# Four column groups of the modulation product: one feature tile and 2048 columns at a time, instead of four feature tiles and 512 columns

## What is computed

```python
mod = jax.nn.silu(c) @ prm['w_ada'][l] + prm['b_ada'][l]
sh1, sc1, g1, sh2, sc2, g2 = jnp.split(mod[:, None, :], 6, axis=-1)
u = x * (1 + sc1) + sh1
...
x = layer_norm(DEEPNORM_ALPHA * x + (1 + g1) * m, ...)
u = x * (1 + sc2) + sh2
```

## Time and profile before

| | us |
|---|---|
| three runs | 1398.95, 1401.20, 1403.52 |
| median | 1401.20 |
| span of the profiled execution (first to last instruction) | 1398.4 |
| TensorE busy in it | 1350.5 (97%) |
| DVE, ACT, POOL busy | 816.9, 572.0, 45.3 |
| 48 loads of `w_ada`, 1 MB each, median time to landing | 7.0 |

### The profile page before, as it was taken

The page is one execution under the profiler, slowest core; times in us unless marked ns, Lnnn a source line. Parts: engine busy times, 40 slices in busy tenths (PEclk is TensorE's granted clock), DMA queues, the critical chain, the costliest instruction groups (busy, mean ns, idle before and its releaser), DMA issues.

```text
span 1398.4 us, 21871 instructions
## 1 busy us (share of the span) xinstructions
PE 1350.5 (97%) x9104; PEld 1132.9 (81%) x9104; DVE 816.9 (58%) x1275; ACT 572.0 (41%) x754; POOL 45.3 (3%) x102
## 2 busy tenths in 40 slices
PE   7999999989999999999999999999999999999996
PEld 3678777879999986788877899999977787877673
DVE  1567216564444446663265843654655668999896
ACT  2361113163433324521232543333344546677762
POOL 6000003000000000000200000000000000000000
PEclk9899999999999999999999899999999999999998
DMA  9643773775544553438342553743756769999991
GB/s 319 209 150 121 249 238 124 252 235 164 169 153 156 174 170 107 150 121 260 107 153 68 188 167 102 223 151 124 223 161 216 228 211 301 316 349 357 332 338 53
DMA packets 205301, 275.87 MB, mean 197 GB/s; under 512 B 7815, under 2 KB 136097, under 8 KB 205204
## 3 DMA queue, kind: packets, MB, share of 16 engines
q1 hardware_dynamic: 193216, 263.62, 57.1%
q10 hardware_dynamic: 11988, 10.86, 2.6%
HBM read 268.16 MB, written 6.30 MB: 196 GB/s over the span
## 4 chain that ended last, share of the span: by engine, by line
PE 92%; DVE 4%; ACT 1%; DMA 1%; issue 1%; SPq 0%; DVEq 0%; ACTq 0%
PE bank L1173 14%; PE bank L981 11%; PE bank L983 11%; PE bank L982 11%; PE bank L1011 7%; PE bank L1013 7%; PE bank L1012 7%; PE bank L1051 4%; PE bank L1122 3%; PE bank L1268 2%; PE bank L1280 2%; PE bank L1137 1%; PE bank L1276 1%; PE bank L1514 1%; PE bank L1085 1%
## 5 line engine op out<-in xcount | busy, mean ns | idle before, releaser
L748 DVE TENSOR_TENSOR lo_raw<-raw,hi 128x2048 fp32r<-128x2048 f32 (+2 forms) x112 | 229.3, 2055 | 99.6 <-ACT hi L1762 60.9
L1762 ACT ACTIVATE hi<-raw 128x2048 fp32r<-128x2048 f32 (+2 forms) x112 | 193.4, 1727 | 113.7 <-PE bank L1013 78.3
L1173 PE MATMUL bank<-UM,raw 128*128 128x288 f32 x864 | 219.4, 410 | 0.0
L981 PE MATMUL bank<-UH,hi 128*128 128x288 f32 x704 | 210.2, 299 | 4.8 <-DVE UL L2178 4.4
L983 PE MATMUL bank<-UL,hi 128*128 128x288 f32 x704 | 207.9, 295 | 0.0
L1173 PEld LDWEIGHTS bank<-UM,raw 128*128 128x128 f32 x864 | 163.3, 192 | 47.4 <-issue 4.6
L2190 DVE TENSOR_TENSOR lo<-raw,hi 128x2048 fp32r<-128x2048 f32 (+1 forms) x42 | 94.1, 2240 | 83.4 <-ACT hi L1975 48.5
L981 PEld LDWEIGHTS bank<-UH,hi 128*128 128x128 f32 x704 | 132.9, 189 | 5.4 <-issue 4.5
L983 PEld LDWEIGHTS bank<-UL,hi 128*128 128x128 f32 x704 | 133.5, 190 | 0.0
L982 PE MATMUL bank<-UH,lo 128*128 128x288 f32 x432 | 128.4, 297 | 0.0
L1011 PE MATMUL bank<-hi,UGH 128*128 128x512 f32 (+9 forms) x288 | 111.7, 388 | 0.0
(11 more groups left out here) (463 smaller groups left out, 2523.8 us busy)
## 6 DMA issues: line engine op xcount, KB each, us to landing
raw<-in_w_ada_dram SPq DMA_DIRECT2D x48, 1024.0 KB, 7.0
raw<-in_w_in_dram SPq DMA_DIRECT2D x28, 1024.0 KB, 8.2
raw<-in_w_exp_gate_dram SPq DMA_DIRECT2D x26, 1024.0 KB, 5.5
raw<-in_w_exp_up_dram SPq DMA_DIRECT2D x26, 1024.0 KB, 7.0
raw<-in_w_exp_down_dram SPq DMA_DIRECT2D x16, 1024.0 KB, 5.1
raw<-in_w_exp_down_dram SPq DMA_DIRECT2D x16, 768.0 KB, 4.8
raw<-in_w_ff_gate_dram SPq DMA_DIRECT2D x11, 1024.0 KB, 5.4
raw<-in_w_ff_up_dram SPq DMA_DIRECT2D x11, 1024.0 KB, 5.3
```

Source lines behind the costliest of these rows:

```text
L748: dve.tensor_tensor(lo_x[g % XRAW][:, 0:XG[g][2] * XG[g][3]], x_raw(g), hi_x[g % XSPLIT][:, 0:XG[g][2] * XG[g][3]].bitcast(F32), ALU.subtr ...
L981: pe.matmul(out, wh, xh, start=start, stop=False)
L1173: mm = pe.matmul(bank[t][:, 0:N], w_[:, d, t * P:t * P + P], UM[:, d, :], start=(d == 0), stop=(d == KT - 1))
L1762: act.activation(hi_x[q][:, 0:XG[g][2] * XG[g][3]], x_raw(g), ACT.Copy).then_inc(S("x_hi_made"), 1)
```

## The change

The column groups now take 512 columns each and the same feature tile. For a block of 2048 columns (four values of c) eight loads bring one feature tile of 128 rows each (rows of 8 KB in HBM); every load gives four products, one for each group, and bank 4 gathers them over all eight loads (four `ada` steps). Then one copy by ACT and one `adaT` of four plain transposes against the identity follow, and four operations of DVE pick the nine values of each group. `ada_ends` says which `ada` step is the last of its block; only it has a copy and an `adaT`.

The first block (layer 0, c 0 to 3) is `paired`: a step loads one half of the features for 512 columns of the shift and the same 512 of the scale, and waits for both loads before its products; two groups take each kind, with different feature tiles. After two steps the partial sums are added and turned by products with `sel2`, two copies of `sel`'s halves beside each other (18 columns), which DVE makes ahead of its first step. The order of the first four is 0, 1, 2, 3, and each pair has one `adaT` behind it.

Since bank 4 is now held across steps, also across the dense network, that network's going down uses the bank pairs (0, 1) and (7, 5). In layer 1 the `ada` step (1,10) moves from behind `lnm` to ahead of the last `wo` block (behind `wo 2`), (1,11) moves from behind `lnv` to its place between `lnm` and `lnv`, and the `adaT` of (1,11) stands behind `lnv` and ahead of `nu`. The number of loads, their bytes and the number of products at L1122 stay.

```diff
@@ -171,2 +171,12 @@
 
+def paired(l, c):
+
+    return (l, c // 4) == (0, 0)
+
+
+def ada_ends(l, c):
+
+    return c % 2 == 1 if paired(l, c) else c % 4 == 3
+
+
 def steps_of():
@@ -175,3 +185,3 @@
     s = [('start',), ('params',)]
-    early = [(0, c) for c in (0, 2, 1, 3, *range(4, ADA_CB))] + [(1, c) for c in range(4)]
+    early = [(0, c) for c in range(ADA_CB)] + [(1, c) for c in range(4)]
     late = [(1, c) for c in range(4, ADA_CB)]
@@ -187,3 +197,4 @@
                 s.append(('ada', *a))
-                last.append(a)
+                if ada_ends(*a):
+                    last.append(a)
 
@@ -329,4 +340,3 @@
         s += [('su', l, 1), ('sm', l, 1), ('wo', l, 2, 0), ('sa', l, 1), ('wo', l, 2, 1)]
-        if l == 0:
-            more_ada()
+        more_ada()
         one('sd_out')
@@ -337,6 +347,3 @@
         flush()
-        if l == 1:
-            more_ada()
         s += [('nu', l, 0), ('u', l, 1)]
-        flush()
         if l == 0:
@@ -373,3 +380,3 @@
     if k == 'ada':
-        return one(4)
+        return one(4) if ada_ends(*step[1:]) else {}
     if k == 'adaT':
@@ -434,2 +441,3 @@
 
+DOWN_BANKS = ((0, 1), (7, 5))
 UP_CB = FF // 256
@@ -545,2 +553,3 @@
         sel = sb("sel", [P, 1 + NSEQ])
+        sel2 = sb("sel2", [P, 2, 1 + NSEQ])
         mask8 = sb("mask8", [P, NSEQ])
@@ -818,6 +827,11 @@
                     for half in range(2):
-                        src = ins['w_ada'][l, half * 512:half * 512 + 512, c * 512:c * 512 + 512]
                         slot = (n + half) % RAW
-                        load(raw[:, slot, :].rearrange("p (k n) -> p k n", k=4),
-                             src.rearrange("(k p) n -> p k n", p=P), ('ada', a + half))
+                        if paired(l, c):
+                            k0, c0 = c % 2 * 512, half * D + c // 2 * 512
+                            src = ins['w_ada'][l, k0:k0 + 512, c0:c0 + 512]
+                            load(raw[:, slot, :].rearrange("p (k n) -> p k n", k=4),
+                                 src.rearrange("(k p) n -> p k n", p=P), ('ada', a + half))
+                        else:
+                            d = 2 * (c % 4) + half
+                            load(raw[:, slot, :], ins['w_ada'][l, d * P:d * P + P, c // 4 * BLK:c // 4 * BLK + BLK], ('ada', a + half))
                 elif k in ('pt', 'wo') and s[3] == 0:
@@ -1115,3 +1129,6 @@
                         pe.wait_ge(read[2], base[2])
-                    fill(base, 4)
+                    c = s[2]
+                    two = paired(l, c)
+                    if c % (2 if two else 4) == 0:
+                        fill(base, 4)
                     for half in range(2):
@@ -1119,8 +1136,18 @@
                         pe.wait_ge(S(f"raw_full{slot}"), 16 * ((n + half) // RAW + 1))
-                        for g in range(4):
-
-                            mm = pe.matmul(bank[4][32 * g:32 * g + 32, :], cT[:, 4 * half + g, :],
-                                           raw[:, slot, g * 512:g * 512 + 512], start=(half == 0), stop=(half == 1))
-                        mm.then_inc(S("ada_used"), 1)
-                        if half == 0 and (l, s[2]) == (0, 1):
+                        if not two:
+                            d = 2 * (c % 4) + half
+                            for g in range(4):
+                                mm = pe.matmul(bank[4][32 * g:32 * g + 32, :], cT[:, d, :], raw[:, slot, g * 512:g * 512 + 512],
+                                               start=(d == 0), stop=(d == KT - 1))
+                            mm.then_inc(S("ada_used"), 1)
+                        elif half == 1:
+                            for d in (0, 2):
+                                for x in range(2):
+                                    for y in range(2):
+                                        at, w_ = 32 * (2 * x + y), raw[:, (n + x) % RAW, (d + y) * 512:(d + y) * 512 + 512]
+                                        mm = pe.matmul(bank[4][at:at + 32, :], cT[:, c % 2 * 4 + d + y, :], w_,
+                                                       start=(c % 2 == 0 and d == 0), stop=(c % 2 == 1 and d == 2))
+                                    if d == 2:
+                                        mm.then_inc(S("ada_used"), 1)
+                        if half == 0 and (l, s[2]) == (0, 2):
                             turn_past(0, base)
@@ -1134,5 +1161,10 @@
                     pe.wait_ge(read[4], base[4])
+                    if base[5] == 0:
+                        pe.wait_ge(S("sel2_made"), 1)
                     fill(base, 5)
                     for j in range(4):
-                        mm = pe.matmul(bank[5][:, 9 * j:9 * j + 9], adas[:, j * P:j * P + P], sel[:, :], start=True, stop=True)
+                        if paired(l, s[2]):
+                            mm = pe.matmul(bank[5][:, 18 * j:18 * j + 18], adas[:, j * P:j * P + P], sel2[:, :, :], start=True, stop=True)
+                        else:
+                            mm = pe.transpose(bank[5][:, j * P:j * P + P], adas[:, j * P:j * P + P], ident[:, :])
                     mm.then_inc(full[5], 1)
@@ -1389,3 +1421,3 @@
 
-                    for b in range(6):
+                    for b in (0, 1, 2, 3, *DOWN_BANKS[1]):
                         fill(base, b)
@@ -1437,3 +1469,3 @@
                                 for t in range(2):
-                                    mm = tiles(None, 4 * c + t, t, m2 + b, DOWN_K[q], HH[:, 8 * q:8 * q + DOWN_K[q], :],
+                                    mm = tiles(None, DOWN_BANKS[c][t], t, m2 + b, DOWN_K[q], HH[:, 8 * q:8 * q + DOWN_K[q], :],
                                                HL[:, 8 * q:8 * q + DOWN_K[q], :], start=(q == 0), stop=(q == 2))
@@ -1802,6 +1834,7 @@
                 elif k == 'ada':
-                    act.wait_ge(S("ada_used"), a + 2)
-                    if (l, s[2]) != (0, 0):
-                        act.wait_ge(full[5], base[5])
-                    act.copy(adas[:, :], bank[4][:, :]).then_inc(read[4], 1)
+                    if ada_ends(l, s[2]):
+                        act.wait_ge(S("ada_used"), a + 2)
+                        if base[5] > 0:
+                            act.wait_ge(full[5], base[5])
+                        act.copy(adas[:, :], bank[4][:, :]).then_inc(read[4], 1)
                 elif k == 'u' and s[2] == 1:
@@ -2193,2 +2226,6 @@
             dve.wait_ge(S("ident_made"), 1)
+            then(dve.memset(sel2[:, :, :], 0.0))
+            for x in range(2):
+                op = dve.tensor_copy(sel2[64 * x:64 * x + 64, x, :], sel[64 * x:64 * x + 64, :])
+            op.then_inc(S("sel2_made"), 1)
 
@@ -2224,6 +2261,13 @@
                     got(base, 5)
-                    kind = c // 2
-                    bias = rep(pT[:, 0, l * 48 + 4 * c:l * 48 + 4 * c + 4], 2, 9)
-                    dve.scalar_tensor_tensor(mod[:, l, 4 * c:4 * c + 4, :], bank[5][:, 0:36].rearrange("p (j s) -> p j s", j=4),
-                                             1.0 if kind in (1, 2, 4, 5) else 0.0, bias, ALU.add, ALU.add).then_inc(read[5], 1)
+                    for x in range(2 if paired(l, c) else 4):
+                        if paired(l, c):
+                            d0 = x * KT + 4 * (c // 2)
+                            src = bank[5][:, 0:72].rearrange("p (j x s) -> p x j s", j=4, x=2)[:, x, :, :]
+                        else:
+                            d0 = c // 4 * 2 * KT + 4 * x
+                            src = bank[5][:, :].rearrange("p (j g s) -> p g j s", j=4, g=4)[:, x, :, 0:9]
+                        bias = rep(pT[:, 0, l * 48 + d0:l * 48 + d0 + 4], 2, 9)
+                        op = dve.scalar_tensor_tensor(mod[:, l, d0:d0 + 4, :], src, 1.0 if d0 // KT in (1, 2, 4, 5) else 0.0,
+                                                      bias, ALU.add, ALU.add)
+                    op.then_inc(read[5], 1)
                 elif k == 'u' and l == 0 and s[2] <= 0:
@@ -2582,3 +2626,3 @@
                         for t in range(2):
-                            last = add_scaled(bank[4 * (cb % 2) + t], 2 * cb + t, l, 5, WTM2[:, t, :])
+                            last = add_scaled(bank[DOWN_BANKS[cb % 2][t]], 2 * cb + t, l, 5, WTM2[:, t, :])
                         last.then_inc(S(f"down_read{cb % 2}"), 1)
```

## The result

| | before | after |
|---|---|---|
| median of the runs, us | 1400.1 (4 runs, 1398.95 to 1403.52) | 1387.6 (4 runs, 1383.9 to 1388.7) |
| span of the profiled execution | 1398.4 | 1382.2 |
| TensorE busy | 1350.5 | 1330.0 |

The ratio is 0.991 with a 95% interval of 0.9891 to 0.993: 12.5 us faster, where 11.3 were forecast, and 1387.6 for 1389.9.

A forecast was written before the change was run, and what follows sets the result against it. TensorE, busy 97% of the span, was taken as the bound. Terms -13.4 - 1.2 + 1.45 + 1.85 = -11.3 us took the span from 1398.4 to 1387.1, carried over to a 1389.9 us median; range 1385 to 1396.

The forecast's parts named there:

- dense work: Seven `adaT` turns amid busy TensorE work disappear, 0.89 us each: 6.2 us saved.
- state rows: Three turns behind the state rows' transposes go, with their waits for bank 5, 1.88 us each: 5.6 us saved.
- those that shrink: Turns of (0,7), (0,11) and (1,7) stay but get shorter, 0.45 us each: 1.35 us saved.
- What reads the price: A turn's cost follows its records, 0.11 us each whether 9 or 128 columns: 0.89 us old, 0.44 us new.
- the rule on overhead: Trainium skill's rule that a matmul costs at least some 60 cycles; by it the sum would be 1.35 us poorer.
- (1,4): Turn ahead of the keys' transposes, mostly covered by a wait for DVE: 0.25 us saved, bounds 0.2 and 0.89.
- the first and the second norm: First layer norm: 1.2 us saved around `lnv` (bounds 0.5 and 1.4); second norm: nothing (bounds -0.4 and +0.4).
- The third norm: Layer 1: (1,10) moves into the busy output projection, costing 1.85 us, and 0.5 comes back; net cost 1.45 us.
- The clock behind the emptied gap: Third norm's emptier gap may lower the clock before the router's products: some 0.7 us lost, kept for the range.
- The start: Paired first block: eight more records wait for the last load at half clock; cost 1.85 us, between 0.9 and 3.
- wait of the solve steps: Rival: steps behind removed turns wait for DVE or ACT instead, giving 1397 us; chance 0.08.
- the late loads: Rival: wide 8 KB-row loads land late in both layers' mixers, TensorE waits 12 us at each, 1414 us; chance 0.04.

The follow-up runs named there:

- e8: Kernel after, with its 20 transposes written as ordinary float32 products with the identity, two records each instead of one: 1389.3 us, ratio 0.9913 to the kernel before.
- e3: The kernel after, unchanged, run once more beside other runs on one chip: 1387.2 us, ratio 0.9907 to the kernel before.
- e4: Kernel after, but layer 1's last 2048 columns made as two pairs, with `ada` steps back in the third norm's gaps: 1383.5 us, ratio 0.988.
- e10: Kernel after, with twelve unread products filling TensorE's gap ahead of the router's products: 1385.4 us, ratio 0.9887 to the kernel before.
- e1: Kernel after, but with the old unpaired first block (layer 0's first 2048 columns): 1391.6 us, ratio 0.9937 to the kernel before.
- e2: Kernel before with only the paired first block added, all later blocks old: 1395.9 us, ratio 0.9969 to the kernel before.
- e5: Kernel after, with one `ada` step per layer moved from dense work into the wait for the keys: 1387.6 us, ratio 0.9908 to the kernel before.
- e7: Kernel after with e4's and e5's edits, plus (1,3) moved behind `lnv` of layer 0's first norm: 1395.2 us, ratio 0.9964 to the kernel before.
- e9: Kernel before, with unread products filling TensorE's waits in the start: 1396.9 us, ratio 0.9967 to the kernel before.
- e11: e4 plus unread products ahead of the keys' squares' sums, the keys' matrix (both layers) and the dense network: 1379.4 us, ratio 0.9841 to the kernel before.
- e12: e11 plus e9's filled start: 1379.1 us, ratio 0.9839 to the kernel before.

## Why the prediction was right, and where not

- **The turns** (dense work, state rows, those that shrink): right in place and almost in size. A turn that goes gave 0.80 and not 0.89. The rows show where the rest is: in after the products of L1300 (128 output columns) start 1.88 us ahead of the `ada` step (112.89 to 114.77), in before the same products started 1.78 ahead of the turn (114.22 to 116.00). So column groups right behind products with 128 columns start 0.1 us later than full products would. Behind the state rows it is the same, 0.53 in place of 0.44. Behind the old turn with its 9 columns there was no such 0.1. It makes 1.0 us over thirteen places; why it is so no run shows.
- **What reads the price**: one record for a transpose and two for a product, by the earlier trace rows and against the rule on overhead that was weighed. e8 bears it out, with 0.1 us for the columns of a whole turn.
- **(1,4), the first and the second norm**: right to 0.1 us. From the first norm's `ada` to `lnv` are 2.22 us in after (272.26 to 274.48), the forecast's 2.2.
- **The third norm**: the step paid again is +1.96 and the sum +1.4 to +1.5, as forecast. The clock behind the emptied gap was kept for the range at 0.7 and measures 2.1 from e3's profile to e4's and 1.9 to 2.2 in e10's times: the term was mis-sized, since all products and transposes of the router slow down (1.18 us and not 0.68 for the first four records), not only the short ones on its chain.
- **The start** is the step that failed: "At that clock eight more records are 1.85 us", and before it that "the first pair's later products cost nothing". It failed in two ways. The first: I read the earlier trace rows as a start that loads and POOL pace, from one wait for POOL and one window with DMA at 1.10. A window in which DMA is fully loaded says that the queue is full, not that anyone waits for it; TensorE's own rows, below, showed 0.15 and 0.27 us for loads and 0.7 for each copy: TensorE was the chain, and pairing takes out two round trips (4.9 us of turns and copies from e1 to e3, less 2.3 of waiting for a load). The second: the 0.50 of the clock behind the last load was no property of the place. In after the sixteen products there took 1.92, in e3 1.89, in e2 3.60. The start measured -4.4 (e1 against e3) where +1.85 stood.

The rows of the start before, which I had and did not weigh:

```profile
20.62 1.06 PE L1137 MATMUL bank<-sel,adas 128*128 128x9 f32 x8 [0.72 <-ACT adas L1806]
...
27.54 1.06 PE L1122 MATMUL bank<-raw,cT 128*32 128x512 f32 x8 [0.15 <-DMA raw<-in_w_ada_dram]
29.31 1.48 PE L1137 MATMUL bank<-sel,adas 128*128 128x9 f32 x8 [0.70 <-ACT adas L1806]
31.06 1.93 PE L1122 MATMUL bank<-raw,cT 128*32 128x512 f32 x8 [0.27 <-DMA raw<-in_w_ada_dram]
```

- **Why the total was still good**: in part by luck. The start gave 6 us more than forecast, the turns 1.0 less, and the router's and the keys' clock took back 3 to 4 that only stood in the range. Two errors of opposite sign met, and the 2.3 us between forecast and result are no measure of how well the start was understood (1.1 of them are the median of before, which moved from 1401.2 to 1400.1 with a fourth run).
- **Rivals**: no wait of the solve steps took the place of a turn, and no wait for `w_ada` arose behind the start. Against the late loads: the 48 loads of `w_ada`, 40 of them now with 8 KB rows, landed 6.6 us after their issue in the median, and 7.0 before.

## What to carry to other kernels

Read what paces a stretch from the waits of the engine that ends it, one by one; a full DMA window or an idle engine is no proof of who is late. Where TensorE idles ahead of dense work, price the work behind it at both of its rates, since moving work out of such a gap can cost more than the work itself (e3 against e4). Unread products in a gap gave 1.9 to 2.2 us at the router and 3.4 at layer 1's squares and keys, but nothing ahead of the dense network, where the next operand came no sooner: faster work pays only until the next wait. And one profile does not tell the rate behind a gap, since executions of the same kernel differ in it. And before a step is moved around a wait, ask whether what ends the wait depends on it (e5), and who stands in line behind its reader (e7).

## What the runs showed that I had not expected

**Half rate with a full clock in the record.** In e1's start sixteen products take 3.64 us and turns 1.88, twice their times elsewhere (1.92 and 1.06), but the window of that stretch in e1 shows a granted clock of 1.00 (behind the five engines' busy times; then DMA share and GB/s):

```profile
16.00:42.00 26.00, 23.03 (x113) 9.71 (x113) 3.26 (x14) 2.65 (x6) 11.78 (x44) 1.00 1.07 362
```

The same holds from 16 to 26 us in after, and from 16 to 20 in before. The Trainium skill, page "TensorE: Matmul & The Clock Gate", section "Seeing it yourself", warns that the clock's trace events are not always to be trusted; here the rows bear it out. That these records ran at 1.2 GHz is read from their lengths, which are those of stretches with a clock of 0.50, and from e9, where the records behind each fill are short; nothing else shows it. In the profile of before the same column reads 0.50 from 31 to 42 us, and there the records are long: it missed the first slow stretch and showed the second. The prediction read it in one window of the second and took the rate there for a property of the place.

**Not tried:** the old, unpaired start, filled, together with e11. Its dense work started at 42.40 in e9 and at 43.89 in e12, so an estimate from these two rows is another 1.5 us at most; e9's lead over e2 at the same place did not last to the end.
